# A bidirectional scan's levels and a convolution's taps regrouped beside 24 weight tiles in a two-block Trainium2 kernel

## What is computed

```python
def conformer_conv(ua, dw_w, dw_b, ln_g, ln_b):      # 31 taps, 256 channels
    a, gate = jnp.split(ua, 2, axis=-1)
    h = a * jax.nn.sigmoid(gate)
    h = depthwise_conv(h, dw_w, dw_b)
    h = layer_norm(h, ln_g, ln_b)
    return jax.nn.silu(h)

def hgrn2_bidir(ub, lb_fwd, lb_bwd, onorm_g):        # 4 heads x 2 directions
    ...
    def step(state, inp):
        qc, lfc, vc = inp
        bcum = jnp.cumsum(lfc, axis=-2)
        kc = -jnp.expm1(lfc)
        o_inter = jnp.einsum('zbhcd,zbhde->zbhce', qc * jnp.exp(bcum), state)
        diff = bcum[..., :, None, :] - bcum[..., None, :, :]
        decay = jnp.exp(diff * mask) * mask
        attn = jnp.sum(qc[..., :, None, :] * kc[..., None, :, :] * decay, axis=-1)
        ...
for l in range(DEPTH):
    u = rms_norm_2(x, g_mix[l]) @ w_in[l]
    ...
    y_a = conformer_conv(ua, ...); y_b = hgrn2_bidir(ub, ...)
    y_c = short_gated_conv(uc, ...); y_d = mla(ud, ...)
```

## Time and profile before

| | |
|---|---|
| three timed runs | 3517.8, 3520.4, 3525.3 us; median 3520.4 |
| the profiled execution | 3519.0 us, its recorded span 3517.2 us |
| PE busy | 3220.4 us, 92% of the span |
| DVE, ACT, POOL busy | 1671.7, 1436.2, 1575.6 us |
| the mixer's loop from the end of tile 9 to the first off_scores | 1872.1 to 1987.27 us, and 2722.1 to 2837.25 us in the second layer |

### The profile page before, as it was taken

The page is one execution under the profiler, slowest core; times in us unless marked ns, Lnnn a source line. Parts: engine busy times, 40 slices in busy tenths (PEclk is TensorE's granted clock), DMA queues, the critical chain, the costliest instruction groups (busy, mean ns, idle before and its releaser), DMA issues. The chain is left out here.

```text
span 3517.2 us, 39165 instructions
## 1 busy us (share of the span) xinstructions
PE 3220.4 (92%) x14620; PEld 2502.2 (71%) x14620; DVE 1671.7 (48%) x2524; ACT 1436.2 (41%) x2281; POOL 1575.6 (45%) x870
## 2 busy tenths in 40 slices
PE   7978899999997899999999968899999986879999
PEld 6655688878765577887878735578887862758877
DVE  2774347731258433774246783433313766443320
ACT  4736433323384553333343444432223344352221
POOL 4623545544563354554465232344445432334444
PEclk8989999999898999999999978999999997889999
DMA  3111233333221122333322101223333200213333
GB/s 111 61 54 43 72 92 100 97 96 98 73 65 54 38 63 94 96 97 98 103 90 79 37 12 42 60 84 97 96 102 97 67 19 18 69 50 98 96 96 102
DMA packets 73740, 265.09 MB, mean 75 GB/s; under 512 B 8656, under 2 KB 9168, under 8 KB 73168
## 3 DMA queue, kind: packets, MB, share of 16 engines
q1 hardware_dynamic: 73552, 262.59, 24.1%
HBM read 260.46 MB, written 2.10 MB: 75 GB/s over the span
## 5 line engine op out<-in xcount | busy, mean ns | idle before, releaser
L359 POOL TENSOR_TENSOR low<-raw,high 128x1024 fp32r<-128x1024 f32 x482 | 1170.3, 2429 | 1299.5 <-ACT high L350 1276.7
L374 PE MATMUL bank<-slot_r,low 128*128 128x512 f32 (+2 forms) x3636 | 1435.2, 395 | 0.0
L375 PE MATMUL bank<-slot_r,high 128*128 128x512 f32 (+2 forms) x3636 | 1432.6, 394 | 0.0
L373 PE MATMUL bank<-slot_r,high 128*128 128x512 f32 (+1 forms) x3316 | 1340.5, 404 | 99.7 <-POOL low L359 22.4
L350 ACT ACTIVATE high<-raw 128x1024 fp32r<-128x1024 f32 x482 | 507.3, 1054 | 848.0 <-PE bank L375 813.9
L373 PEld LDWEIGHTS bank<-slot_r,high 128*128 128x128 f32 x3316 | 637.1, 192 | 286.8 <-issue 69.5
L374 PEld LDWEIGHTS bank<-slot_r,low 128*128 128x128 f32 (+1 forms) x3636 | 696.6, 192 | 149.0 <-issue 9.4
L375 PEld LDWEIGHTS bank<-slot_r,high 128*128 128x128 f32 (+1 forms) x3636 | 695.9, 191 | 149.7
L1568 DVE SCALAR_TENSOR_TENSOR tmp<-padded,small,tmp 128x512 f32<-128x512 f32 x176 | 210.0, 1252 | 0.0
L834 POOL TENSOR_SCALAR tmp<-tmp,stat 128x512 f32<-128x512 f32 (+3 forms) x128 | 71.6, 559 | 193.8 <-DVE stat L809 170.0
L698 PE MATMUL bank<-slots 64*128 64x256 f32 (+4 forms) x384 | 95.8, 508 | 44.5 <-PEq L320 40.7
(11 more groups left out here) (308 smaller groups left out, 3751.3 us busy)
## 6 DMA issues: line engine op xcount, KB each, us to landing
raw<-w SPq DMA_DIRECT2D x482, 512.0 KB, 3.6
slots<-x_in SPq DMA_DIRECT2D x4, 512.0 KB, 6.5
slots<-mem_in SPq DMA_DIRECT2D x2, 1024.0 KB, 4.9
out<-slots SPq DMA_DIRECT2D x8, 256.0 KB, 4.5
const<-const_in SPq DMA_DIRECT2D x1, 1073.5 KB, 10.6
padded<-p_in SPq DMA_DIRECT2D x2, 512.0 KB, 4.9
tmp<-masks_in SPq DMA_DIRECT2D x1, 512.0 KB, 11.4
small<-small SPq DMA_DIRECT2D x2, 231.5 KB, 2.7
```

Of the source, the lines that this page charges most:

```text
L359: pool.tensor_tensor(self.low[:, t % PARTS, :], self.raw[:, t % RING, :], self.high[:, t % PARTS, :].bitcast(F32), ALU.subtract).then_inc( ...
L373: pe.matmul(acc, lhs[0], rhs[1], start=first, stop=False)
L374: pe.matmul(acc, lhs[1], rhs[0], start=False, stop=False)
L375: return pe.matmul(acc, lhs[0], rhs[0], start=False, stop=last)
```

## The change

The halves are handed out two at a time, so a whole level follows each of the tiles 9 to 16, and tiles 17 to 23 have no scores behind them. The taps become one a tile for j = 13 to 16 and seven a tile for j = 17 to 23, 53 by tile 23. Of the nine that are left, four stay behind the scaled pieces, three and two stand in the first two query heads, and no tap stands after the heads.

```diff
         def halves_after(j):
 
-            first = j - FIRST_HALF_AT
-            if first < 0:
-                return []
-            return HALVES[first:first + 1] if j < N - 1 else HALVES[first:]
+            first = 2 * (j - FIRST_HALF_AT)
+            return HALVES[first:first + 2] if first >= 0 else []
...
                     if j >= AT_GA + 3:
-                        taps(3 if j < 19 else 5)
+                        taps(7 if j > 16 else 1)
```

## The result

| | before | after |
|---|---|---|
| median of the timed runs | 3519.6 us | 3584.9 us (3584.1 to 3587.1) |
| ratio of after to before | | 1.0185, 95% interval 1.0173 to 1.0198 |
| span of the profiled execution | 3517.2 us | 3585.3 us |
| first mixer, end of tile 9 to the mixer's end | 219.8 us | 256.2 us |
| second mixer, the same | 219.8 us | 255.9 us |

The forecast was 3579 us in a range of 3552 to 3602.

A forecast was written before the change was run, and what follows sets the result against it. PE was taken to bound the loop before, DVE its end; a loop 34.0 us longer less 4.1 given back made 29.9 us a mixer, 60 for two, on 3519: 3579 us, range 3552 to 3602.

The forecast's parts named there:

- waits inside the levels: Tiles 9 to 16: PE waits for banks to be copied out within a whole level, 17.8 us a mixer.
- clock, tiles 9 to 17: Half clock after the waits at levels 3 and 4, charged twice at 1.6 us: 3.2 us a mixer.
- end of tile 9 to end of tile 17: First stretch of the loop: 77.0 us of PE work plus 17.8 of waits and 3.2 of clock, 98.0 us.
- end of tile 17 to off_scores: Plain-tile stretch, paced by DVE's evacuations, taps, six subtractions sat out and scaled pieces: 51.2 us.
- given back behind the loop: Ten taps fewer behind the loop: 2.07 us ahead of the layer norm plus 2.0 beside the heads, 4.1 us.
- sum over before: Net cost of a mixer: loop 34.0 us longer, less 4.1 given back, 29.9 us.
- C: Time from a tile's end to its level's first copy, 5.0 us at levels 3 and 4; loss about C - 0.25.
- The first rival: Plain tiles: POOL's subtractions cost DVE's taps nothing, PE keeps its pace; 18.5 us a mixer, 3556 us; 7%.
- The rule of reading ACT's idle time: Heads: ACT idled only 1.96 us ahead of its root, so the chain comes at most 2 us earlier.
- PE doesn't wait inside the levels: Masked levels: copies keep up, 21.0 us of waiting and clock fall away; 8.9 us a mixer, 3537 us; 5%.
- faster: Heads gain 11.4 us a mixer while both first rivals hold in the loop; 3499 us; 3%.
- Worse: Every level's wait drops the clock, and DVE and POOL delay each other 2.7 us; 41 a mixer, 3601 us; 12%.

The follow-up runs named there:

- d_filled: The changed kernel with matmuls whose result nobody reads put into PE's waits of levels 0 to 5; 3572.6 us, 1.0153 of the kernel before.
- c_copies_first: The changed kernel with a level's masked copies moved ahead of row product, total and next keys in DVE's queue; 3552.3 us, 1.0095 of the kernel before.
- e_short: The changed kernel with POOL's subtraction beside tiles 18 to 23 cut to 128 of 1024 columns; 3565.4 us, 1.0125 of the kernel before.
- b_taps: The kernel before with only the new taps, half a level still behind each tile; 3523.4 us, 1.0016 of the kernel before.

## Why the prediction was right, and by how much each term was off

For the first mixer, us:

| term | predicted | measured | by |
|---|---|---|---|
| waits inside the levels | 17.8 | 18.3 | d_filled: 95.26 less 77.0 of work |
| clock, tiles 9 to 17 | 3.2 | 7.4 | changed kernel less d_filled |
| end of tile 9 to end of tile 17 | 98.0 | 102.6 | trace after |
| end of tile 17 to off_scores | 51.2 | 51.4 | trace after |
| given back behind the loop | 4.1 | 2.5 | trace after and before |
| sum over before | +29.9 | +36.4 | |

**The waits.** They stood where they were forecast, 4.21 and 4.14 us at levels 3 and 4 against 4.4, with C = 4.8 against 5.0 at level 3, and c_copies_first shows that DVE's order makes them. The bookkeeping was sound because every C came from a row in which the same instructions stood in the same order.

**The clock** is the term that was mis-sized: 3.2 us forecast, 7.4 and 6.7 measured. The prediction charged it to the two waits over 4 us and left the waits of 2 us out, though the earlier trace rows showed a fall after 2.17. Set beside d_filled, from one evacuation to the next, levels 1 to 5 of the first mixer lost 1.5, 1.6, 0.9, 1.8 and 1.6 us, together the 7.4, and levels 0, 6 and 7 nothing. In the second mixer level 5 lost nothing either, behind the same two waits of 1.09 and 0.67 us. PE's last quarter of level 5, in the first mixer and in the second:

```profile
1946.13 2.01 PE L1756 MATMUL bank<-slots 64*128 64x128 f32 x16 [0.67 <-ACT PT L1894]
...
2831.09 1.16 PE L1756 MATMUL bank<-slots 64*128 64x128 f32 x16 [0.67 <-ACT PT L1894]
```

c_copies_first has these two waits as well, with the clock at 1.00. So the length of a wait does not by itself tell whether a fall follows. That the waits of levels 1 to 4 were followed by one in both mixers is what the traces show; why, they leave open.

**The plain tiles.** 51.2 against 51.4: six subtractions at 2.17. The evacuations in the middle of the stretch are 7.3 to 7.4 us apart, as forecast, but the wait ahead of off_scores was 13.15 us and not 15 to 18: another 4.6 us of PE's waiting stood at the starts of three plain tiles (1.39, 1.61 and 1.55 us). e_short took them away and with them 11.2 us. The first rival, that the lock costs nothing, would have had that gain without an edit.

**The heads.** The last three taps gave their 2.0 us and the heads gave 2.0. DVE's timeline after, from the first head's product to the first long reciprocal:

```profile
2067.74 0.69 DVE L2165 TENSOR_TENSOR tmp<-bank,const 96x512 f32<-96x512 f32 x1 [3.60 <-PE bank L1864]
...
2085.03 3.35 DVE L2172 RECIPROCAL tmp<-tmp 96x512 f32<-96x512 f32 x1 [2.75 <-ACT tmp L1988]
```

That is 17.3 us, against 19.3 before (2047.29 less 2027.96), and DVE now waits there for ACT. The rule of reading ACT's idle time ahead of the row one hopes to pull forward held. What was missed is on the other side: the stretch from off_scores to the first head took 41.8 us instead of 40.7, and the clock stayed low for longer in it. The stretch from 4.7 to 8.7 us after the start of off_scores, after and before:

```profile
2030.60:2034.60 4.00, 4.00 (x6) 1.85 (x6) 0.00 (x0) 2.32 (x4) 0.00 (x0) 0.50 0.00 0
```

```profile
1992.00:1996.00 4.00, 4.00 (x8) 1.60 (x9) 0.24 (x1) 2.89 (x5) 0.00 (x0) 0.72 0.00 0
```

How long the clock stays low there does not follow the length of the wait. With a wait of 7.33 us e_short was still at 0.50 from 8 to 10 us after the start of off_scores and took 42.3 us to the first head; b_taps, with 9.96 us, was back at 1.00 by then and took 41.2. The remaining 0.4 lie behind the norm.

**The rivals.** "PE doesn't wait inside the levels" and "faster" needed copies that keep up; they nearly do in c_copies_first, where DVE's order is another, and even that kernel is slower than before, since merging halves saves only 1.5 us of PE's work while the plain tiles still lack room for seven taps. "Worse" had the right mechanism for the clock, at five levels of its seven in the first mixer and four in the second.

**The total.** In the traces the two mixers cost 12.7 us more than forecast: 7.7 for the clock (7.4 + 6.7 against 6.4), 3.6 for the smaller gift (2.5 and 2.1 against 4.1 each), the rest spread over the waits and the plain tiles. Unchanged code took 4.4 us less. That the forecast of 3579 lies only 6 us under the median of 3584.9 owes something to that.

## What to carry to other kernels

Grouping work that goes through few buffers turns a wait that was hidden under other work into a wait in the open; ask what the draining engine has to do ahead of the first drain, and put that behind it. Spare time of an engine counts where it lies: the 18.6 us that DVE had free in the loop were no help beside 5.46 us tiles, while 15 taps fitted free of charge into its idle times behind the loop. And before moving work beside a plain matmul stream, add to its own length what the other engine's instructions on the same port will shut it out for.

## What the runs showed of the hardware that was not expected

- The clock fell behind a wait of 1.61 us inside level 2, in both mixers, and stayed at 1.00 behind one of 1.61 us between plain tiles. Filling the waits with useless matmuls made the kernel 11 us faster with 110 matmuls more.
- A subtraction on POOL beside back-to-back two-tensor instructions of DVE delays the group by its length less about 0.25 us (0.21 for 0.48 us, 2.17 for 2.40), and masked copies from PSUM hardly: the eight at 1873.75 took 5.27 us beside a subtraction that lasted from 1873.20 to 1876.05, and the four at 1914.68, with none beside them, 2.52, so that eight took at most 0.2 us more.
